# Attention scores on two row halves of TensorE, with keys stored once instead of twice with zeros

## The reference

```python
# MoBA, 8 heads; with 256 tokens there is one block, so only s_own counts
s_own = jnp.einsum('bhqd,bhld->bhql', qc, k_own).astype(jnp.float32) * scale
s_own = jnp.where(kpos[None, :] <= qpos[:, None], s_own, -jnp.inf)
# stick breaking, 8 heads, query blocks of 128
z = jnp.einsum('bhtd,bhsd->bhts', qf[:, :, t0:kn], kf[:, :, :kn]) * scale
# sliding window of 128, 16 query heads over 4 key heads, with bias and sinks
logits = jnp.einsum('bqhgd,bkhd->bhgqk', qn, kn) * scale + bias
```

## Time and profile before

| | |
|---|---|
| median of 3 runs | 1534.68 us (1534.47 to 1539.3) |
| the profiled execution | 1534.6 us |
| its span, first to last instruction | 1532.8 us |
| PE busy | 1373.2 us (90%) |
| DVE, ACT, POOL busy | 1032.0, 710.8, 577.2 us |

### The profile page before, as it was taken

The page is one execution under the profiler, slowest core; times in us unless marked ns, Lnnn a source line. Parts: engine busy times, 40 slices in busy tenths (PEclk is TensorE's granted clock), DMA queues, the critical chain, the costliest instruction groups (busy, mean ns, idle before and its releaser), DMA issues.

```text
span 1532.8 us, 18254 instructions
## 1 busy us (share of the span) xinstructions
PE 1373.2 (90%) x5985; PEld 964.9 (63%) x5985; DVE 1032.0 (67%) x1920; ACT 710.8 (46%) x1378; POOL 577.2 (38%) x541
## 2 busy tenths in 40 slices
PE   7999989768878877887779999999999999999998
PEld 6887954323333332333337878798888778888887
DVE  5885869666666666666655558658863686598734
ACT  5545634322223333223325463477645655776534
POOL 3040654433333433333334422055433512364514
PEclk9999999998998899899999999999999999999999
DMA  9297699999999999999998510567665433476650
GB/s 316 89 176 249 255 381 390 421 422 421 422 422 421 421 422 421 422 422 421 421 422 303 193 60 2 164 192 204 190 210 198 162 136 89 137 207 195 215 186 28
DMA packets 180739, 414.99 MB, mean 271 GB/s; under 512 B 9178, under 2 KB 113218, under 8 KB 148418
## 3 DMA queue, kind: packets, MB, share of 16 engines
q0 software_dynamic: 37440, 268.45, 42.4%
q1 hardware_dynamic: 143090, 145.66, 30.8%
q10 hardware_dynamic: 144, 0.04, 0.0%
HBM read 409.93 MB, written 4.19 MB: 270 GB/s over the span
## 4 chain that ended last, share of the span: by engine, by line
PE 51%; DMA 21%; DVE 10%; ACT 7%; POOL 6%; issue 5%; ACTq 0%; POOLq 0%; DVEq 0%
DMA expert_rows<-in_peer_uv,route_idx 19%; PE ps L2554 10%; PE ps L2377 9%; PE ps L2091 8%; PE ps L2093 7%; PE ps L2092 7%; PE ps L2555 5%; POOL expert_rows L642 2%; POOL weights_lo L593 2%; ACT weights_hi L440 2%; DMA work_b<-in_peer_uv,route_idx 2%; DVE weights_lo L447 2%; PE ps L2056 1%; DVE expert_rows L1670 1%; ACT scratch L967 1%
## 5 line engine op out<-in xcount | busy, mean ns | idle before, releaser
L1670 DVE CUSTOM_DVE_ANT_0 expert_rows<-expert_rows,ps 128x1024 f32<-128x1024 f32 x180 | 219.5, 1221 | 131.3 <-DMA expert_rows<-in_peer_uv,route_idx 130.0
L2377 PE MATMUL ps<-expert_rows,proj 128*128 128x512 f32 x496 | 236.8, 634 | 65.7 <-ACT proj L967 65.7
L642 POOL DMA_INDIRECT expert_rows<-in_peer_uv,route_idx x191 | 192.0, 1005 | 266.2 <-PE ps L2377 208.0
L593 POOL TENSOR_TENSOR weights_lo<-weights_raw,weights_hi 128x512 fp32r<-128x512 f32 x116 | 153.4, 1356 | 351.8 <-ACT weights_hi L440 309.9
L440 ACT CAST weights_hi<-weights_raw 128x2048 fp32r<-128x2048 f32 x98 | 185.5, 1917 | 105.9 <-PE ps L2093 83.0
L2377 PEld LDWEIGHTS ps<-expert_rows,proj 128*128 128x128 f32 x496 | 97.8, 202 | 203.8 <-issue 118.6
L2554 PE MATMUL ps<-x_normT,weights_hi 128*128 128x512 f32 x640 | 222.5, 394 | 0.0
L447 DVE TENSOR_TENSOR weights_lo<-weights_raw,weights_hi 128x2048 fp32r<-128x2048 f32 x69 | 163.2, 2373 | 60.6 <-ACT weights_hi L440 60.2
L953 ACT ACTIVATE proj<-proj 128x4 f32<-128x4 f32 x64 | 13.1, 205 | 405.3 <-DVE proj L1670 405.2
L2091 PE MATMUL ps<-weights_hi,x_normT 128*128 128x512 f32 (+1 forms) x496 | 188.3, 380 | 8.7 <-DVE weights_lo L447 3.1
L2093 PE MATMUL ps<-weights_hi,x_normT 128*128 128x512 f32 (+1 forms) x496 | 184.8, 373 | 0.0
(11 more groups left out here) (371 smaller groups left out, 2421.6 us busy)
## 6 DMA issues: line engine op xcount, KB each, us to landing
weights_raw<-in_ffn_up SPq DMA_DIRECT2D x88, 512.0 KB, 5.0
weights_raw<-in_ffn_down SPq DMA_DIRECT2D x22, 1024.0 KB, 4.9
weights_raw<-in_ab_w_in SPq DMA_DIRECT2D x14, 1024.0 KB, 5.8
weights_raw<-in_w_in SPq DMA_DIRECT2D x12, 1024.0 KB, 7.7
weights_raw<-in_ple_gate SPq DMA_DIRECT2D x8, 1024.0 KB, 6.2
weights_raw<-in_c_w_in SPq DMA_DIRECT2D x6, 1024.0 KB, 5.5
weights_raw<-in_w_out SPq DMA_DIRECT2D x4, 1024.0 KB, 12.6
weights_raw<-in_peer_w_query SPq DMA_DIRECT2D x4, 1024.0 KB, 11.9
```

The lines of the kernel that those rows point to most:

```text
L593: ins = pool.tensor_tensor(w.lo[:, c], w.raw[:, c], w.hi[:, c].bitcast(F32), ALU.subtract)
L642: nc.gpsimd.indirect_dma_start(out=dst, out_offset=None, in_=table, in_offset=bass.IndirectOffsetOnAxis(ap=r_idx[:, q, n:n + 1], axis=0)). ...
L1670: ins = nc.vector.tensor_tensor_reduce(out=rows, in0=rows, in1=tokens, scale=1.0, scalar=0.0, op0=ALU.mult, op1=ALU.add, accum_out=r_dot[: ...
L2377: ins = pe.matmul(PS[:, (J[f"peer_{t}"] + m) % 8, :], DIAG[b][:, k, :], rows[:, m * BANK:(m + 1) * BANK], start=False, stop=False, skip_gr ...
```

## The change

KT holds each key once: pair v of heads on 128 partitions, even head on 0 to 63, odd head on 64 to 127. A score matmul takes 64 partitions of queries and of keys. Two banks are written in turns, even heads to the first and odd heads to the second, so a bank holds every other head, and the instructions that empty the banks write with a stride over heads (`alternate`). The copies of the keys are two instead of four in each place. The dense tiles, the DMAs, the jobs and the order of the jobs are the same.

```diff
-        KZT = B[:, 0:2048].rearrange("p (v t) -> p v t", v=8)
+        KT = B[:, 0:1024].rearrange("p (v t) -> p v t", v=4)
+        def alternate(per, m):
+            first = 2 * per * (m // 2) + m % 2
+            return slice(first, first + 2 * per - 1, 2)
...
-                    for par in range(2):
-                        d = KZT[:, 4 * m:4 * m + 4, :].rearrange("p (c h) t -> p c h t", h=2)[:, :, par, :]
-                        ins = nc.scalar.activation(d, PS[:, (j + m) % 8, :].rearrange("p (c t) -> p c t", c=2), ACT.Copy,
-                                                   scale=const("head_rows")[:, par:par + 1])
-                    ins.then_inc(evac_done, 1)
+                    act.copy(KT[:, 2 * m:2 * m + 2, :], PS[:, (j + m) % 8, :].rearrange("p (c t) -> p c t", c=2)).then_inc(evac_done, 1)
...
-                    d = PB[u % 2][:, m * BANK:(m + 1) * BANK].rearrange("p (h s) -> p h s", h=per)
+                    d = heads[:, alternate(per, m), :]
...
-                key_pairs(J["mb_T"] + 2, 2, KZT)
+                transposed(J["mb_T"] + 2, 2, KT)
...
-                key_pairs(J["sb_T"] + 2, 2, KZT)
+                transposed(J["sb_T"] + 2, 2, KT)
...
-                for m in range(8 // per):
-                    b = bank(j + m)
-                    for h in range(per):
-                        hh = m * per + h
-                        ins = pe.matmul(b[:, h * cols:(h + 1) * cols], queries[:, pair(hh), t * P:(t + 1) * P],
-                                        KZT[:, variant(hh), 0:cols], start=True, stop=True)
-                    ins.then_inc(pe_done, 1)
+                for m in range(0, 8 // per, 2):
+                    two = [bank(j + m), bank(j + m + 1)]
+                    for n in range(2 * per):
+                        hh, rows = m * per + n, slice(n % 2 * HD, (n % 2 + 1) * HD)
+                        ins = pe.matmul(two[n % 2][:, n // 2 * cols:(n // 2 + 1) * cols], queries[rows, pair(hh), t * P:(t + 1) * P],
+                                        KT[rows, variant(hh), 0:cols], start=True, stop=True)
+                        if n // 2 == per - 1:
+                            ins.then_inc(pe_done, 1)
```

More of the change, by code:

```diff
@@ L308, in build @@
         ZL0 = A[:, 0:2048].rearrange("p (g n) -> p g n", g=2)
+        SB_FIRST = A[:, 0:2048].rearrange("p (h t) -> p h t", h=8)
         L1 = SCR[:, 0:1024].rearrange("p (h t) -> p h t", h=8)
@@ L1473, in logits @@
                 v.wait_ge(evac_done, j)
+                heads = PB[u % 2][:, 0:8 * cols].rearrange("p (h s) -> p h s", h=8)
                 for m in range(8 // per):
                     src = bank(j + m).rearrange("p (h s) -> p h s", h=per)
-                    d = PB[u % 2][:, m * BANK:(m + 1) * BANK].rearrange("p (h s) -> p h s", h=per)
-                    freed(nc.vector.scalar_tensor_tensor(out=d, in0=src, scalar=HD ** -0.5, in1=add(m * per, per, cols),
+                    d = heads[:, alternate(per, m), :]
+                    freed(nc.vector.scalar_tensor_tensor(out=d, in0=src, scalar=HD ** -0.5, in1=add(alternate(per, m), per, cols),
                                                          op0=ALU.mult, op1=ALU.add), j + m, m == 8 // per - 1)
@@ L1504, in attended, with causal @@
                 freed(nc.vector.tensor_tensor(dst.rearrange("p (h n) -> p h n", h=8), src, bc(den, HD), ALU.mult), jo, True)
-            def causal(h0, n, cols):
+            def causal(heads, n, cols):
                 return bc(causal_add[:, 2 * P - cols:2 * P], n, 1)
@@ L1798, in sb_logits @@
                     add = bc(C[:, at_add:at_add + cols], heads, 1)
-                    z, src = (x.rearrange("p (h t) -> p h t", h=heads) for x in (A[:, m * BANK:(m + 1) * BANK], bank(j)))
+                    src = bank(j).rearrange("p (h t) -> p h t", h=heads)
+                    z = (SB_FIRST if m < 4 else Z1)[:, alternate(heads, m % 4), :]
                     freed(nc.vector.scalar_tensor_tensor(out=z, in0=src, scalar=HD ** -0.5, in1=add, op0=ALU.mult, op1=ALU.add), j, True)
@@ L2002, in window_logits, with biased @@
                 t, g = u % 2, u // 2
-                def biased(h0, n, cols):
-                    return BIAS[:, 8 * g + h0:8 * g + h0 + n, 2 * P - cols:2 * P]
+                def biased(heads, n, cols):
+                    return BIAS[:, 8 * g + heads.start:8 * g + heads.stop:2, 2 * P - cols:2 * P]
                 logits(J[f"sw_L{u}"], t, biased, sink=slice(8 * g, 8 * g + 8))
@@ L2260, in moba_logits @@
             def moba_logits(t):
-                logits(J[f"mb_L{t}"], t, lambda h: h // 2, lambda h: h, SQT)
+                logits(J[f"mb_L{t}"], t, lambda h: h // 2, lambda h: h // 2, SQT)
             def moba_out(t):
@@ L2413, in _ @@
             pe.wait_ge(evac_done, END["sb_T"])
[L2414 to L2425, removed]
+            for m, per, first in ((0, 2, 0), (2, 2, 0), (4, 4, P)):
+                two = [bank(J["sb_Z"] + m), bank(J["sb_Z"] + m + 1)]
+                cols = S - first
+                for n in range(2 * per):
+                    h, rows = m % 4 * per + n, slice(n % 2 * HD, (n % 2 + 1) * HD)
+                    ins = pe.matmul(two[n % 2][:, n // 2 * cols:(n // 2 + 1) * cols], KT[rows, h // 2, first:first + P],
+                                    SQT[rows, h // 2, first:S], start=True, stop=True)
+                    if n // 2 == per - 1:
+                        ins.then_inc(pe_done, 1)
             for n in range(3, 5):
@@ L2642, in window_logits @@
                 pe.wait_ge(evac_done, END[f"sw_Q{g}"])
-                logits(J[f"sw_L{u}"], t, lambda h: (8 * g + h) // 2, lambda h: ((8 * g + h) // 4) * 2 + h % 2)
+                logits(J[f"sw_L{u}"], t, lambda h: (8 * g + h) // 2, lambda h: (8 * g + h) // 4)
             def window_T(u):
```

## The result

The changed kernel takes 1540.32 us (median of 20 runs, 1534.64 to 1544.96), the kernel before 1535.9 us in the same series (20 runs, 1534.17 to 1539.3): ratio 1.0029, 95% interval 1.0021 to 1.0038. It is slower, by some 4.4 us, and above the range. The fastest runs of the two are alike; what differs is how often a run is slower than that, and with the time goes the mean granted clock: 0.971 in the fastest run of the changed kernel, 0.962 to 0.965 in the four slowest. The profiled execution took 1541.98 us, its span is 1540.2.

What follows compares the result with a forecast made beforehand. Scores were taken to end last only in MoBA, and barely; DVE bounds the window's later part. 1534.6 - 0.13 (key copies) + 0.0 (matmuls) = 1534.5 us, range 1533.0 to 1537.0, chance 0.45.

Steps and rivals of the forecast that it cites:

- Step 1: Two key copies instead of four: DVE's 1.4 us, twice, hidden in waits; ACT's in the window gain 0.13 us.
- Step 2: Score matmuls on row halves in MoBA, stick breaking and window: 0.0 us, with ends of -0.2 and +0.6 in MoBA.
- first bound: Row halves overlap fully, so 16 score passes take the time of 8, 0.90 us.
- rival A: Halves do not overlap for 128 columns, so MoBA's scores cost +0.6 us: 1535.1 us; chance 0.28.
- The switch: Changing the array shape between full-row and half-row matmuls costs TensorE about 0.17 us each time.
- Rival C: ACT's last copy in the window's unit 2 truly waits for scores: 1.0 us more gain, 1533.3 us; chance 0.10.
- rival B: Clock falls in TensorE's longer waits: one stall, behind the window's unit 3, gives 1536.3 us, three places 1539.8; chance 0.17.
- the fall of the gather stage: Rival B's price: after TensorE stood still 2.7 us there, 3.5 us at half speed, 1.75 us less work.
- The signs named in advance: Wrong if clock below 1.00 between 800 and 1500 us, DVE bank wait over 0.5 us, or copies above 0.7 us.

Runs made afterwards that it cites:

- 9 fillers: Changed kernel with 9 instead of 3 filler matmuls behind the window's units 1 and 3: ratio 1.0008 (0.9991 to 1.0026).
- 7 fillers: Two runs of the changed kernel with 7 instead of 3 filler matmuls: behind the window's units 1 and 3, ratio 1.0028; behind unit 3 alone, 1.0026.
- four copies: Changed kernel with DVE's key copies in MoBA and stick breaking in four pieces instead of two: 1538.96 us (one run).
- unit 1 without fillers: Kernel before, on full rows, without the 3 filler matmuls behind the window's units 1 and 3: ratio 1.0029 (1.0018 to 1.004).
- the window as before: Row halves in MoBA and stick breaking alone, the sliding window on full rows as in the kernel before: ratio 1.000 (0.9985 to 1.0015).
- one half after the other: Changed kernel, but of each two banks first all even heads, then all odd ones, instead of in turns: ratio 1.0031 (1.0016 to 1.0047).

## Why the prediction was wrong

**What bounds the kernel.** Right: in stick breaking and the window the scores did not end last, and in MoBA they did so only just (DVE still waits 0.36 us for them). With their time halved DVE's first copy came 0.2 us later in MoBA (93.37 - 0.61 against 92.56) and 0.2 earlier in the window, by ACT's doing.

**Step 1, key copies.** Right in size: two take 1.29 us on DVE (88.25 in the trace after) and 1.24 on ACT. Hidden as said, DVE's waits in front of the dense tile's result are 2.73 and 4.00 us for the 2.7 and 4.0 forecast. DVE's start behind the keys came at 1248.63 - 3.50 = 1245.13 (forecast 1245.10), with 3.50 the lateness at the stage's start; the root at 1251.41 - 3.50 = 1247.91, not 1248.06, so the gain was 0.22 to 0.28, not 0.13. What step 1 missed is DVE's pause of 0.18 us in the MoBA tail, a loss of 0.25: the two cancel.

**Step 2, the matmuls.** The halves overlap in full: two passes of 128 columns, one on either half, start some 7 ns apart, and a pair takes 0.112 us, what one pass took the earlier trace rows. So the first bound held and rival A fell, and with it the row of line 2255 as a guide. Here the Trainium skill's rule (TensorE: Matmul & The Clock Gate, Part 3), that a pack takes about as long as one matmul, agrees with the trace: 0.112 us against 0.113. The switch cost about what was forecast (0.17): at each entry from a dense tile the weight loads stand idle for 0.35 us, but the first score matmul starts only 0.09 us later behind the last one of the tile than before (0.32 against 0.23), and the second pair 0.10 us later behind the first than the pairs after it, 0.19 in all. MoBA came out at the 0.0 forecast, in part by luck: the 91.54 that was taken for the start of the scores is a row of the chain, while the timeline has TensorE start them at 91.38 (91.47 after, without the 0.61); DVE began at 92.76 and not at 92.63; and its two copies then took 1.29 us and not 1.42. The copies with a stride take 0.65 us each, so nothing was lost by the stride.

**Rival C** fell as argued: ACT's four copies in unit 2 take 2.60 us as before, with the scores halved.

**The step that failed** is the weight and price of rival B. The waits were forecast well (3.7 us, measured 3.33 and 3.62), and so was it that the fall behind unit 1 is covered. Wrong was the sentence "it is one fall behind one wait that the rows show, and the new waits are not all that long", which gave it 0.17: the fall behind unit 3 was in all six profiles with row halves everywhere and a wait there of 1.89 us or more. Wrong was also the price: I took the fall of the gather stage, 3.5 us at half speed, 1.75 us of work. Behind unit 3 half speed held for 10.2 us, over passes of 64 columns and transposes that are the path: 3.92 us and the 0.24 gained before it, so 4.2. Why a fall came behind unit 3 each time, and not behind every wait of that length, stays open. And the 1.7 us more of waiting that step 2 gave stick breaking were put down as harmless, where they cost 1.6 us when the clock fell behind them. With 3.9 for the window alone the rival's sum would have been 1538.4, and the range would have had to reach beyond 1540. A smaller part of the miss is the base: of the 5.8 us between 1534.5 and 1540.32, 1.2 are there because the kernel before had a median of 1535.9 us in the series of 20, and not the 1534.68 of three runs. Nor was 0.3% the limit of what a measurement tells: the 20 runs put the ratio between 1.0021 and 1.0038.

The signs named in advance did their work: a clock below 1.00 between 800 and 1500 us was the first of those that were to prove the forecast wrong.

## What to carry to other kernels

An engine made faster off the path still pays for the time that it then stands still: before an edit that shortens TensorE's work in front of a wait, look up what follows the wait, and price half speed over that work and not over the nearest fall in the trace: here it held for 10.2 us, three times the fall of the gather stage. If the saved matmuls were on no path, fill the wait again, to below what it was: in the profiles here 9 fillers did it, 7 did not. A loss that some executions have and others do not, with a lower mean clock in the longer ones, points to such falls and not to the edit's own work.

## What the runs showed of the hardware

How long a fall lasts differs by place: 3.4 us over dense tiles of 512 columns (128.5, 894.6), 10.2 to 13.7 us over the 64-column passes and transposes behind unit 3. TensorE was busy for all of the 10.1 us from 1278.90 on, and the clock stayed at 0.50. What runs in it does not settle the length: behind unit 1, over transposes, fillers and 64-column passes, it was 3.4 us in the profile after, 6.8 with four copies and 10.2 with halves in the window only. The 32 passes take 6.55 us at 0.50 against 3.68 at 1.00, 0.20 us a pass against 0.115, so what paces them slows down with the clock.

The length of a wait does not settle whether a fall follows: none behind 2.80 us (at 97 us in the profile after) or 2.62 us (unit 1 without fillers), one behind 1.78 us in stick breaking, and, with the window as before and with one half after the other, one even at MoBA's wait of 1.20 us (108 us), 9 us behind a longer wait. In the profiles without a fall there the same wait of 1.20 us is found as well, and the wait of 2.00 us in the MoBA tail goes both ways in two executions of one kernel. And a fall need not cost anything: behind the wait of 2.80 us at 97 us the clock fell in four other profiles (the second of the changed kernel, both with 7 fillers, four copies), and nothing was lost by it there.

The passes of one row half do not wait for those of the other that were issued ahead of them. With all even heads ahead of the odd ones, the first pass of the odd half began 0.55 us after the first of the even half (1254.895 and 1254.341), while three even passes issued ahead of it were still to start. So the halves overlap in part, and 32 passes took 3.44 us, between the 2.89 of halves in turns and the 5.40 of full rows. The Trainium skill (TensorE: Matmul & The Clock Gate, Part 3) has matmuls start strictly in their order; these starts differ.

DVE paused 0.18 us in mid-stream for no wait that the profile shows, in all nine profiles with two instructions fewer ahead of it, and in none of the five with the old number. What causes it was not tested.
